# A two-layer decoder trunk on one core: boundary work reordered, level differences moved to VectorE

## The chip, the core and the metric

The kernel runs on one core of one Trainium2 chip. The metric is device time in microseconds (us), lower is better. The core has five engines that run side by side, each through its own list of instructions in order: TensorE (PE: matrix products into PSUM), VectorE (DVE), ScalarE (ACT), GpSimd (POOL) and SyncE (SP, which here only issues DMAs). They wait for each other by semaphores; `wait_ge(s, n)` holds an engine until `s` has reached `n`.

## The reference

Everything is float32. Batch 1, 512 tokens, width 1024, two layers. Cut to what matters:

```python
for l in range(2):
    mod = (silu(c) @ w_ada[l] + b_ada[l]).reshape(1, 3, 3, 1024)      # shift, scale, gate of 3 sub-layers
    x = modulated_sublayer(x, ffn1,         norm_g[l,0], norm_g[l,1], mod[:,0], 0.5)
    x = modulated_sublayer(x, token_mixing, norm_g[l,2], norm_g[l,3], mod[:,1], 1.0)
    x = modulated_sublayer(x, ffn2,         norm_g[l,4], norm_g[l,5], mod[:,2], 0.5)

def modulated_sublayer(x, fn, g_pre, g_post, m, res_w):
    h = rms_norm(x, g_pre) * (1 + scale) + shift
    return x + res_w * gate * rms_norm(fn(h), g_post)
def swiglu_ffn(h, w_in, w_out):                                        # hidden width 2816
    a, b = split(h @ w_in, 2);  return (silu(a) * b) @ w_out
# token_mixing: h @ w_in (8832 columns), then three mixers, gates, h @ w_out.
# Mixer A (6 heads): a gated linear recurrence with decays exp(b[t] - b[s]).
```

## The kernel before, in words

**Precision.** Each float32 factor is split into a high part (rounded) and a low part (the rest), and one product becomes three on PE: high by high, low by high, high by low (`three`, lines L769 to L771). So each group of weights (2048 columns on 128 partitions, 1 MB) is loaded into `RAW[g % 2]`, rounded by ACT into `WH[g % 2]` (`high`, L1164; in quarters L1173) and subtracted by DVE into `WL[g % 2]` (`low`, L1562; in quarters L1573). SP loads group g when the low part of group g - 2 has been made. `used(g)` counts that PE has done with a group; `free(g)` says which `used` the rounding of group g waits for.

**FFN.** The first product has 22 groups (11 pairs i, with u = 0, 1) of 128 hidden columns each. Groups 0 and 1 are done together by `first_pair`, in two halves of 256 tokens; each later group is 48 products of 512 columns. When PE has done a group, ACT takes silu (L1272), DVE multiplies (L1597), makes the low part of the group two further on (L1562), and of the result (L1601); this is a *tile* (`ffn_tile`). PE's group n + 2 waits for the low part and for the gate made in tile n. The second product (`rows_product`) has 11 groups; it fills all eight PSUM banks, and its last two groups are done together, column by column, so that finished columns can go on.

**Modulation.** `mod` is a product with a single row, so it is done beside the FFNs: the 1024 rows of a 512-column chunk of `w_ada` come in eight transfers of 256 KB into four buffers `AW`, DVE sums them up into `AACC` (*pieces*: four instructions, L1610 and L1613, for each half chunk), PE adds up the partitions with four products by ones (`ada`, L832), DVE copies the result (L1620). FFN1 of a layer has 11 chunks, one for each pair of groups; FFN2 has 7 in layer 0 and 2 in layer 1. On SP the transfers of the pieces of tile n stand behind the loads of group n + 3, which wait for the low part that is made in tile n - 1.

**Boundary.** Between two sub-layers (five times, and a last one without a next input) the output is squared (ACT L1198, DVE adds pairs L1482), summed over partitions by PE with ones (L779), the root taken by ACT (`root`, L1179 and L1181), the residual added by DVE (L1494, L1498), the new x squared (ACT L1206) and summed (PE L786), its root taken, and the next input made (DVE `U` L1505, ACT `HH` L1211, DVE `HL` L1512), in two halves of the tokens, so that PE can begin with the first columns. So that the next weights can be rounded before PE is done with the last rows, the first two groups behind a boundary go into two extra pairs of buffers, `WXH` and `WXL` (`beside`, `halves_of`).

**Mixing.** After the pair of `first_pair` 35 more items of the input product, each in eight steps k = 0..7; each step has some products and beside them a step of a mixer. Head h of mixer A has its eight steps in the item of head h + 1: for each of seven levels POOL makes a difference (`AD`, L1968), ACT the exponentials (`AE`, L1325 and L1326), DVE the scaled factors (`KL` L1737, `QL` L1739), PE a product (L973), and DVE takes it up (`AS`, L1721). Then `merge` (4 groups) and the 4 groups of `w_out` by `rows_product`.

The order is written out by hand in each engine's program; nothing is scheduled by a planner.

## Time and profile before

| | |
|---|---|
| Time, median of 3 runs | 3120.86 us (3119.76 to 3122.25) |
| Profiled execution: its own time | 3121.1 us |
| Profiled execution: span of the instructions | 3119.3 us |
| PE busy | 2929.9 us, 94% of the span |
| DVE busy | 1541.3 us, 49% |
| ACT busy | 1005.0 us, 32% |
| POOL busy | 193.1 us, 6% |
| mean granted clock of TensorE | 0.975 of full |

PE is busy nearly all the time, so the time is what PE has to do plus the stretches in which it waits. The clock is granted at one of two levels, full (2.4 GHz) and half (1.2 GHz); "0.975" is a mean over the span. A group of the profile's rows names the line, the engine, the operation and output <- inputs, with busy time and mean duration; idle time of an engine is put down to what ended it.

### The profile page before, as it was taken

The page shows a single profiled execution, that of the slowest core. Times are in us where ns is not written, and L with a number is a line of the kernel's source. Part 1 is how long each engine was busy: PE and PEld are TensorE (multiplying, and loading weights), DVE is VectorE, ACT ScalarE, POOL GpSimd, SP SyncE. Part 2 cuts the span into 40 slices and gives each one's busy share as a digit, 9 for nine tenths or more (in the row PEclk, how much of TensorE's full clock was granted, in tenths as well). Part 3 has the DMA queues.
Part 4 walks back from the last instruction along what each step waited for, and adds up shares of the span by engine and source line. Part 5 has one row for each costly group of instructions (what it writes and reads, how often), then busy time and mean ns, then how long its engine had stood idle before and what let it go on. Part 6 is the DMA issues. An engine that isn't in the chain of part 4 may idle for free.

```text
span 3119.3 us, 40607 instructions
## 1 busy us (share of the span) xinstructions
PE 2929.9 (94%) x16999; PEld 2558.1 (82%) x16999; DVE 1541.3 (49%) x2236; ACT 1005.0 (32%) x1455; POOL 193.1 (6%) x188
## 2 busy tenths in 40 slices
PE   6999898989999988999989989899899999899998
PEld 5888897777788788889988879877777887888897
DVE  5555236777344446542255552477753554453323
ACT  3322124444422323222242221354443232332212
POOL 1000001221100020000000000021211002000000
PEclk7999999999999999999999999999999999999999
DMA  6555331222112233542226542222111232343321
GB/s 238 176 189 189 109 96 61 61 62 68 41 55 82 81 127 104 189 135 95 97 88 195 186 167 89 88 62 75 51 52 41 68 95 81 109 122 95 102 89 55
DMA packets 358854, 324.53 MB, mean 104 GB/s; under 512 B 12300, under 2 KB 305552, under 8 KB 357776
## 3 DMA queue, kind: packets, MB, share of 16 engines
q1 hardware_dynamic: 357136, 319.77, 32.4%
q8 instruction: 135, 2.21, 0.3%
q10 hardware_dynamic: 1536, 2.16, 0.2%
q14 instruction: 47, 0.39, 0.0%
HBM read 313.43 MB, written 6.29 MB: 102 GB/s over the span
## 4 chain that ended last, share of the span: by engine, by line
PE 85%; DVE 7%; ACT 3%; issue 2%; POOL 0%; ACTq 0%; DVEq 0%; POOLq 0%
PE PS L769 25%; PE PS L771 24%; PE PS L770 24%; PE PS L973 2%; PE PS L786 2%; DVE WL L1573 1%; PE PS L1048 1%; PE PS L1010 1%; PE PS L1070 1%; PE PS L1034 1%; PE PS L1025 1%; PE PS L1022 1%; PE PS L832 1%; ACT WH L1164 1%; PE PS L779 1%
## 5 line engine op out<-in xcount | busy, mean ns | idle before, releaser
L769 PE MATMUL PS<-HH,WH 128*128 128x512 f32 (+1 forms) x2512 | 974.3, 388 | 27.3 <-DVE WL L1562 10.3
L771 PE MATMUL PS<-HH,WL 128*128 128x512 f32 (+1 forms) x2512 | 948.7, 378 | 0.0
L770 PE MATMUL PS<-HL,WH 128*128 128x512 f32 (+1 forms) x2512 | 946.9, 377 | 0.0
L1562 DVE TENSOR_TENSOR WL<-RAW,WH 128x2048 fp32r<-128x2048 f32 x142 | 325.5, 2292 | 515.5 <-ACT WH L1164 515.5
L769 PEld LDWEIGHTS PS<-HH,WH 128*128 128x128 f32 x2512 | 475.7, 189 | 116.7 <-DVE WL L1573 13.7
L771 PEld LDWEIGHTS PS<-HH,WL 128*128 128x128 f32 x2512 | 475.0, 189 | 88.7
L770 PEld LDWEIGHTS PS<-HL,WH 128*128 128x128 f32 x2512 | 476.1, 190 | 82.0 <-issue 2.9
L1164 ACT ACTIVATE WH<-RAW 128x2048 fp32r<-128x2048 f32 x142 | 271.8, 1914 | 792.6 <-PE PS L771 792.6
L769 PE MATMUL PS<-GH,WH 128*128 128x256 f32 x1408 | 405.0, 288 | 18.2 <-DVE WL L1562 17.5
L771 PE MATMUL PS<-GH,WL 128*128 128x256 f32 x1408 | 403.7, 287 | 0.0
L770 PE MATMUL PS<-GL,WH 128*128 128x256 f32 x1408 | 403.3, 286 | 0.0
L769 PEld LDWEIGHTS PS<-GH,WH 128*128 128x128 f32 x1408 | 272.1, 193 | 19.6 <-DVE WL L1562 18.4
L771 PEld LDWEIGHTS PS<-GH,WL 128*128 128x128 f32 x1408 | 271.3, 193 | 0.0
L770 PEld LDWEIGHTS PS<-GL,WH 128*128 128x128 f32 x1408 | 270.9, 192 | 0.4
L1573 DVE TENSOR_TENSOR WL<-RAW,WH 128x512 fp32r<-128x512 f32 (+1 forms) x264 | 173.4, 685 | 145.0 <-ACT WH L1173 144.5
L1597 DVE TENSOR_TENSOR SB<-SB,PS 128x512 f32<-128x512 f32 x88 | 60.5, 687 | 336.2 <-PE PS L771 336.2
L1613 DVE SCALAR_TENSOR_TENSOR AACC<-AW,CC,AACC 128x512 f32<-128x512 f32 x217 | 162.9, 751 | 20.8 <-DVE AACC L1613 0.9
L1173 ACT ACTIVATE WH<-RAW 128x512 fp32r<-128x512 f32 (+1 forms) x264 | 145.9, 601 | 82.9 <-PE PS L771 53.1
L1272 ACT ACTIVATE SB<-PS 128x512 f32<-128x512 f32 x88 | 52.7, 599 | 266.0 <-PE PS L771 261.0
L769 PE MATMUL PS<-HH,WXH 128*128 128x256 f32 x320 | 98.5, 308 | 23.4 <-DVE HL L1512 23.4
L1968 POOL TENSOR_TENSOR AD<-AB 128x512 f32<-128x512 f32 x84 | 97.1, 1173 | 184.0 <-ACT AE L1326 103.9
L973 PEld LDWEIGHTS PS<-QL,KL 128*64 128x64 f32 (+6 forms) x672 | 76.0, 177 | 38.2 <-DVE QL L1739 29.1
(225 smaller groups left out, 3470.3 us busy)
## 6 DMA issues: line engine op xcount, KB each, us to landing
RAW<-in_ffn_w_in SPq DMA_DIRECT2D x176, 512.0 KB, 5.2
RAW<-in_w_in SPq DMA_DIRECT2D x132, 512.0 KB, 4.7
AW<-in_w_ada SPq DMA_DIRECT2D x248, 256.0 KB, 4.8
RAW<-in_ffn_w_out SPq DMA_DIRECT2D x88, 512.0 KB, 4.2
AWB<-in_w_ada SPq DMA_DIRECT2D x5, 2048.0 KB, 16.0
RAW<-in_w_out SPq DMA_DIRECT2D x16, 512.0 KB, 4.0
x_kept<-X SPq DMA_DIRECT2D x2, 2048.0 KB, 7.4
X<-x_kept SPq DMA_DIRECT2D x2, 2048.0 KB, 10.1
```

The lines of the kernel that those rows point to most:

```text
L769: pe.matmul(o, ah, bh, start=start, stop=skip, skip_group_check=skip)
L770: pe.matmul(o, ah, bl, start=False, stop=skip, skip_group_check=skip)
L771: return pe.matmul(o, al, bh, start=False, stop=stop or skip, skip_group_check=skip)
L786: mm = pe.matmul(y_at(half, 0), ones, XSQ[q][:, e, :], start=(q == 0 and e == 0), stop=True, skip_group_check=True)
L973: mm = pe.matmul(PS[0:keys, 2 + n % 2, c * 64:(c + 1) * 64], KL[n % 2][:, c * P:c * P + keys], QL[n % 2][:, c, :], start=True, stop=True)
L1164: act.activation(halves_of(g)[0][:, 0:n], RAW[g % 2][:, 0:n], ACT.Copy).then_inc(w_high, 1)
L1173: act.activation(WH[slot][:, q * n:(q + 1) * n], RAW[slot][:, q * n:(q + 1) * n], ACT.Copy).then_inc(w_high if q == 3 else part_high, 1)
L1562: dve.tensor_tensor(wl[:, 0:n], RAW[g % 2][:, 0:n], wh[:, 0:n].bitcast(F32), ALU.subtract).then_inc(w_low, 1)
L1573: ins = dve.tensor_tensor(WL[slot][:, part], RAW[slot][:, part], WH[slot][:, part].bitcast(F32), ALU.subtract)
L1597: dve.tensor_tensor(SB[u][:, :], SB[u][:, :], PS[:, 2 * u + 1, :], ALU.mult).then_inc(gated, 1)
L1613: ins = dve.scalar_tensor_tensor(acc, w, CC[:, k:k + 1], acc, ALU.mult, ALU.add)
L1968: pool.tensor_tensor(level_view(AD[n % 2][:, :], k), b, b[:, :, w // 2 - 1:w // 2].broadcast_to([P, SEQ // w, w]), ALU.subtract).then_inc( ...
```

## The change

1. **The extra buffers** `WXH` and `WXL` now hold the last two groups of each `rows_product` (`beside`: `g % NG in HALVED`) and no longer the first two groups behind a boundary. Both last groups may be rounded from the use of the fourth last on. The third group behind a boundary (`g + 2`) now waits for the use of the first (in `first_pair`), where it waited for the end of the rows.
2. **Rows.** The first group of `rows_product` goes through the PSUM banks in another order, and each quarter waits only for its own banks. The columns of `ada` take banks 4 and 5 in turn.
3. **Modulation.** `ada(i)` stands behind group (i, 1) of its own pair i, where it stood one pair later (`ada(0)` behind group (1, 0)). On DVE the pieces of a tile stand in front of the tile, where they stood behind it.
4. **Boundary.** On ACT the squares of x come one step earlier among the squares of y; the second root of y is taken behind the first two columns of the next input. On PE the second sums of x come at steps 3, 4, 5, 5 of the first half, where they came at steps 4 to 7.
5. **Merging.** The low part of the first branch group is made in the last item, not behind it.
6. **Level differences.** The 84 differences `AD` are made by DVE and no longer by POOL; level k + 1 is made in step k.

SP's list of instructions is the same. PE has the same products, in another order.

```diff
@@ -439,12 +439,12 @@
     def beside(g):
-        return g % NG in (G_MIX, G_MIX + 1, G_FFN2, G_FFN2 + 1) or (g % NG < 2 and now[0] + g // NG > 0)
+        return g % NG in HALVED
     def free(g):
         if beside(g):
-            back = max((e for e in ROW_ENDS if e <= g), default=0) - 3
+            back = min(e for e in ROW_ENDS if e > g) - 4
         else:
@@ -809,8 +809,10 @@
                                 mm.then_inc(done(i), 1)
-                            if not half and p and (u, i) == (1, 1) and k >= KT // 2:
-                                x_sum(p, 1, k - KT // 2)
+                            if not half and p and (u, i) == (1, 1) and 3 <= k <= 5:
+                                x_sum(p, 1, k - 3)
+                                if k == 5:
+                                    x_sum(p, 1, 3)
                 def ffn_in(p, f, g0):
@@ -827,9 +829,9 @@
                         pe.wait_ge(ada_part, at(ada_part, i * KT + (ADA_BEFORE[f] + 2) * KT))
-                        pe.wait_ge(ada_out, at(ada_out, ADA_BEFORE[f] + i))
+                        pe.wait_ge(ada_out, at(ada_out, max(ADA_BEFORE[f] + i - 1, 0)))
                         for q in range(4):
-                            mm = pe.matmul(PS[:, 4, q:q + 1], AACC[i % 2][:, q * P:(q + 1) * P], ones[:, 0:1],
+                            mm = pe.matmul(PS[:, 4 + i % 2, q:q + 1], AACC[i % 2][:, q * P:(q + 1) * P], ones[:, 0:1],
                                            start=True, stop=True)
@@ -839,17 +841,16 @@
                             group(u)
-                            if u and i <= n:
-                                ada(i - 1)
-                    if n == FI // 2:
-                        ada(FI // 2 - 1)
-
-                def rows_product(g0, n, rh, rl, ready, b, bank_free=None):
+                            if (i, u) == (1, 0):
+                                ada(0)
+                            if u and i < n:
+                                ada(i)
+
+                def rows_product(g0, n, rh, rl, ready, b, bank_free):
                     def column(i, j, half):
-                        wh = WH[(g0 + i) % 2][:, :].rearrange("p (k c) -> p k c", k=2)
-                        wl = WL[(g0 + i) % 2][:, :].rearrange("p (k c) -> p k c", k=2)
+                        wh, wl = (w[:, :].rearrange("p (k c) -> p k c", k=2) for w in halves_of(g0 + i))
                         cols = HALVES[half]
@@ -859,9 +860,9 @@
                         ready(i)
-                        for half in (1, 0) if i == 0 else (0, 1):
-                            for j in range(KT):
-                                if i == 0 and bank_free:
+                        for half, j0 in ((1, 4), (0, 0), (0, 4), (1, 0)) if i == 0 else ((0, 0), (0, 4), (1, 0), (1, 4)):
+                            for j in range(j0, j0 + 4):
+                                if i == 0 and j == j0:
                                     bank_free(half, j)
@@ -899,6 +900,8 @@
                     def bank_free(half, j):
+                        if (half, j) == (1, 4):
+                            pe.wait_ge(x_done, at(x_done, 8 * b))
                         if half and j == 0:
@@ -1127,9 +1130,10 @@
                             mm.then_inc((br_done, w_used)[u], 1)
+                def merged_free(half, j):
+                    pe.wait_ge(br_mul, at(br_mul, {(1, 4): KT - 2, (0, 0): KT - 1}.get((half, j), KT)))
+
                 def merged(i):
-                    if i == 0:
-                        pe.wait_ge(br_mul, at(br_mul, KT))
                     pe.wait_ge(m_low, at(m_low, 2 * i + 2))
@@ -1146,7 +1150,7 @@
                     merge()
-                    rows_product(G_WO, 4, lambda k: HH[:, k, :], lambda k: HL[:, k, :], merged, 3 * l + 1)
+                    rows_product(G_WO, 4, lambda k: HH[:, k, :], lambda k: HL[:, k, :], merged, 3 * l + 1, merged_free)
                     ffn_in(3 * l + 2, 1, G_FFN2)
@@ -1239,14 +1243,16 @@
                         square_y(b, 1, q)
-                        if q in (1, 2) and not last:
-                            square_x(b + 1, 0, 2 * q - 2)
-                            square_x(b + 1, 0, 2 * q - 1)
-                    root_y(b, 1)
+                        if q < 2 and not last:
+                            square_x(b + 1, 0, 2 * q)
+                            square_x(b + 1, 0, 2 * q + 1)
                     if last:
+                        root_y(b, 1)
                         return
...
                         input_high(b + 1, 0, j)
+                        if j == 1:
+                            root_y(b, 1)
                         if j in (2, 4, 6, 7):
@@ -1582,13 +1588,13 @@
                         for u in range(2):
-                            ffn_tile(f, g0, i, u)
-                            if u == 0 and 1 < i <= n + 1:
-                                ada_columns(f, i - 2)
                             if i < n:
                                 ada_pieces(f, i, u)
-                    for i in range(min(n, FI // 2 - 2), n):
-                        ada_columns(f, i)
+                            ffn_tile(f, g0, i, u)
+                            if u == 0 and 1 <= i <= n:
+                                ada_columns(f, i - 1)
+                    if n == FI // 2:
+                        ada_columns(f, n - 1)
                 def ffn_tile(f, g0, i, u):
@@ -1617,7 +1623,7 @@
                     ch = i + ADA_FIRST if f == 0 else i + ADA_ALL - ADA_OWN if i < ADA_OWN else i - ADA_OWN
-                    dve.tensor_copy(MOD[:, 4 * ch:4 * ch + 4], PS[:, 4, 0:4]).then_inc(ada_out, 1)
+                    dve.tensor_copy(MOD[:, 4 * ch:4 * ch + 4], PS[:, 4 + i % 2, 0:4]).then_inc(ada_out, 1)
                 def take(m, i):
@@ -1713,6 +1719,16 @@
                         dve.tensor_tensor_scan(AB[h % 2][:, :], const("reset"), AB[h % 2][:, :], 0.0, ALU.mult, ALU.add).then_inc(p_log, 1)
+                def a_diff(h, k):
+
+                    n = A_LEVELS * h + k
+                    dve.wait_ge(p_log, at(p_log, 3 * h + 3))
+                    dve.wait_ge(v_decay, at(v_decay, max(n - 1, 0)))
+                    w = P >> k
+                    b = level_view(AB[h % 2][:, :], k)
+                    dve.tensor_tensor(level_view(AD[n % 2][:, :], k), b,
+                                       b[:, :, w // 2 - 1:w // 2].broadcast_to([P, SEQ // w, w]), ALU.subtract).then_inc(v_diff, 1)
+
                 def level_out(h, k):
@@ -1726,6 +1742,10 @@
                     aq, ab, ak, s = AQ[h % 2], AB[h % 2], AK[h % 2], AS[h % 2]
+                    if k == 0:
+                        a_diff(h, 0)
+                    if k + 1 < A_LEVELS:
+                        a_diff(h, k + 1)
                     if k < A_LEVELS:
@@ -1924,9 +1944,10 @@
                                 low_part(m + 1, k - 1)
+                            if (m, k) == (NM - 1, 3):
+                                low(G_BR)
                             mixers(m, k)
                     take(NM - 1, 1)
-                    low(G_BR)
                     low(G_BR + 1)
@@ -1958,25 +1979,12 @@
             def _(pool):
-                def a_diff(h, k):
...
                         pool.tensor_tensor(QB[h % 2][:, :], AQ[h % 2][:, :], AK[h % 2][:, :], ALU.mult).then_inc(i_qk, 1)
-                    if k < A_LEVELS:
-                        a_diff(h, k)
-
                 def mixers(m, k):
```

The next two pieces are DVE's rows in FFN1 of layer 0, pair i = 1: `SB` is the gated product of a tile, `WL` the weights' low part, `GL` the result's; `AACC<-AW` are the pieces of a chunk. Before:

```order
L1597 TENSOR_TENSOR SB_73<-SB_73,PS 128x512 [waits w_used,silu_done]
L1562 TENSOR_TENSOR WL_56<-RAW_52,WH_54 128x2048 [waits w_high]
L1601 TENSOR_TENSOR GL<-SB_73,GH 128x512 [waits g_high]
L1610 TENSOR_SCALAR AACC_80<-AW_75,CC 128x512 [waits ada_sum,ada_in0]
L1613 SCALAR_TENSOR_TENSOR AACC_80<-AW_76,CC,AACC_80 128x512 [waits ada_part,ada_in1]
L1613 SCALAR_TENSOR_TENSOR AACC_80<-AW_78,CC,AACC_80 128x512 [waits ada_part,ada_in2]
L1613 SCALAR_TENSOR_TENSOR AACC_80<-AW_79,CC,AACC_80 128x512 [waits ada_part,ada_in3]
L1597 TENSOR_TENSOR SB_74<-SB_74,PS 128x512 [waits w_used,silu_done]
L1562 TENSOR_TENSOR WL_57<-RAW_53,WH_55 128x2048 [waits w_high]
L1601 TENSOR_TENSOR GL<-SB_74,GH 128x512 [waits g_high]
L1613 SCALAR_TENSOR_TENSOR AACC_80<-AW_75,CC,AACC_80 128x512 [waits ada_part,ada_in0]
```

and now:

```order
L1616 TENSOR_SCALAR AACC_80<-AW_75,CC 128x512 [waits ada_sum,ada_in0]
L1619 SCALAR_TENSOR_TENSOR AACC_80<-AW_76,CC,AACC_80 128x512 [waits ada_part,ada_in1]
L1619 SCALAR_TENSOR_TENSOR AACC_80<-AW_78,CC,AACC_80 128x512 [waits ada_part,ada_in2]
L1619 SCALAR_TENSOR_TENSOR AACC_80<-AW_79,CC,AACC_80 128x512 [waits ada_part,ada_in3]
L1603 TENSOR_TENSOR SB_73<-SB_73,PS 128x512 [waits w_used,silu_done]
L1568 TENSOR_TENSOR WL_56<-RAW_52,WH_54 128x2048 [waits w_high]
L1607 TENSOR_TENSOR GL<-SB_73,GH 128x512 [waits g_high]
L1626 COPY MOD<-PS 128x4 [waits ada_sum]
L1619 SCALAR_TENSOR_TENSOR AACC_80<-AW_75,CC,AACC_80 128x512 [waits ada_part,ada_in0]
L1619 SCALAR_TENSOR_TENSOR AACC_80<-AW_76,CC,AACC_80 128x512 [waits ada_part,ada_in1]
L1619 SCALAR_TENSOR_TENSOR AACC_80<-AW_78,CC,AACC_80 128x512 [waits ada_part,ada_in2]
L1619 SCALAR_TENSOR_TENSOR AACC_80<-AW_79,CC,AACC_80 128x512 [waits ada_part,ada_in3]
```

The four pieces stood behind `SB`, `WL` and `GL` of their tile, and now stand in front of them; so `WL` for the group two further on stands behind waits for four transfers (`ada_in0` to `ada_in3`).

ACT at the boundary between FFN1 and mixing (`YSQ` and `XSQ` are the squares of y and x, `NLN` and `NR_103` the root for y, `NR_104` that for x, `HH` the next input, `WXH` the extra buffers). Before:

```order
L1198 ACTIVATE YSQ<-PS 128x2x256 [waits y_done] x2
L1206 ACTIVATE XSQ_93<-X 128x512 [waits n2_mm,x_done]
L1206 ACTIVATE XSQ_94<-X 128x512 [waits n2_mm,x_done]
L1198 ACTIVATE YSQ<-PS 128x2x256 [waits y_done]
L1206 ACTIVATE XSQ_95<-X 128x512 [waits n2_mm,x_done]
L1206 ACTIVATE XSQ_96<-X 128x512 [waits n2_mm,x_done]
L1179 ACTIVATE NLN<-PS,EPSC 128x256 [waits n2_mm]
L1181 ACTIVATE NR_104<-NLN 128x256 [waits n2_ln]
L1198 ACTIVATE YSQ<-PS 128x256 [waits y_done]
L1179 ACTIVATE NLN<-PS,EPSC 128x256 [waits n1_mm]
L1181 ACTIVATE NR_103<-NLN 128x256 [waits n1_ln]
L1211 ACTIVATE HH<-U,MOD 128x256 [waits u_done] x3
```

and now:

```order
L1202 ACTIVATE YSQ<-PS 128x2x256 [waits y_done]
L1210 ACTIVATE XSQ_93<-X 128x512 [waits n2_mm,x_done]
L1210 ACTIVATE XSQ_94<-X 128x512 [waits n2_mm,x_done]
L1202 ACTIVATE YSQ<-PS 128x2x256 [waits y_done]
L1210 ACTIVATE XSQ_95<-X 128x512 [waits n2_mm,x_done]
L1210 ACTIVATE XSQ_96<-X 128x512 [waits n2_mm,x_done]
L1202 ACTIVATE YSQ<-PS 128x2x256 [waits y_done]
L1183 ACTIVATE NLN<-PS,EPSC 128x256 [waits n2_mm]
L1185 ACTIVATE NR_104<-NLN 128x256 [waits n2_ln]
L1202 ACTIVATE YSQ<-PS 128x256 [waits y_done]
L1215 ACTIVATE HH<-U,MOD 128x256 [waits u_done] x2
L1183 ACTIVATE NLN<-PS,EPSC 128x256 [waits n1_mm]
```

Each two squares of x (`XSQ`) stand one square of y earlier, and the second root for y (`NLN` and then `NR_103`) stands behind the first two `HH`.

DVE in the first steps of head 0 of mixer A (`AD` the differences, `KL` and `QL` the scaled factors), now; before, no `AD` stood in DVE's rows:

```order
L1729 TENSOR_TENSOR AD_125<-AB_115 128x512 [waits v_decay,p_log]
L1729 TENSOR_TENSOR AD_126<-AB_115 128x512 [waits v_decay,p_log]
L1757 TENSOR_TENSOR KL_129<-AK_117,AE_127 128x4x64 [waits p_k,kl_set,p_q,v_mm,v_decay]
L1759 TENSOR_TENSOR QL_131<-AQ_113,AE_127 128x256
L1767 TENSOR_TENSOR KD<-AB_115 128x512 [waits i_turn,p_log]
L1771 TENSOR_TENSOR AS_133<-PS,CT 128x512 [waits i_o,i_diag]
L1579 TENSOR_TENSOR WL_57<-RAW_53,WH_55 128x256 [waits part_high,i_s0]
L1729 TENSOR_TENSOR AD_125<-AB_115 128x512 [waits v_decay,p_log]
L1757 TENSOR_TENSOR KL_130<-AK_117,AE_128 128x8x32 [waits p_k,p_q,v_mm,v_decay]
L1759 TENSOR_TENSOR QL_132<-AQ_113,AE_128 128x256
L1776 TENSOR_TENSOR QB_135<-AQ_113,EB 128x512 [waits i_eb]
```

Two differences stand ahead of the first factors, and then one ahead of each level's.

## Rows read from the trace of the kernel before

**Rows 1.** The page, busy time of each engine.

```profile
PE 2929.9 (94%) x16999; PEld 2558.1 (82%) x16999; DVE 1541.3 (49%) x2236; ACT 1005.0 (32%) x1455; POOL 193.1 (6%) x188
```

**Rows 2.** Who waited for whom, PE, 95 to 3119: total us, times, longest us.

```profile
PE PS L769 <- DVE WL L1562: 34.2, 9, 4.4
PE PS L769 <- DVE HL L1512: 23.4, 11, 2.6
PE PS L973 <- DVE AS L1721: 18.8, 12, 2.0
PE PS L832 <- DVE MOD L1620: 15.2, 2, 7.6
PE PS L786 <- ACT XSQ L1206: 12.1, 10, 1.2
...
PE PS L769 <- issue: 6.6, 2, 3.3
```

**Rows 3.** PE in order of time, four places.

```profile
330.49 1.84 PE L832 MATMUL PS<-CT,AACC 128*128 128x1 f32 x8 [7.60 <-DVE MOD L1620]
...
480.75 0.36 PE L769 MATMUL PS<-HH,WXH 128*128 128x256 f32 x1 [2.02 <-DVE HL L1512]
...
1072.97 0.77 PE L769 MATMUL PS<-YH,WH 128*128 128x512 f32 x1 [3.19 <-DVE WL L1562]
...
1380.69 0.47 PE L769 MATMUL PS<-HH,WH 128*128 128x512 f32 x1
```

**Rows 4.** Busy us by stretch; the column after POOL is granted clock.

```profile
442.30:450.30 8.00, 7.97 (x47) 7.98 (x48) 2.30 (x1) 3.39 (x4) 0.00 (x0) 0.67 0.90 260
...
3075.30:3083.30 8.00, 7.98 (x54) 7.98 (x55) 0.00 (x0) 1.56 (x3) 0.00 (x0) 0.79 0.00 0
330.50:340.50 10.00, 9.65 (x53) 9.60 (x54) 0.76 (x6) 0.00 (x0) 0.00 (x0) 0.61 0.33 120
1858.90:1868.90 10.00, 9.65 (x63) 9.60 (x64) 0.76 (x6) 0.00 (x0) 0.00 (x0) 0.74 0.32 119
1073.00:1081.00 8.00, 8.00 (x23) 6.35 (x24) 2.29 (x1) 0.00 (x0) 0.00 (x0) 0.63 0.79 262
480.80:488.80 8.00, 7.97 (x53) 7.68 (x54) 7.89 (x19) 2.92 (x7) 0.00 (x0) 0.79 0.00 1
500.20:508.20 8.00, 8.00 (x67) 8.00 (x68) 6.50 (x14) 5.47 (x8) 0.00 (x0) 1.00 0.00 0
```

**Rows 5.** SP in order of time, FFN1 of layer 0: issues of transfers.

```profile
95.64 1.00 SPq L688 DMA_DIRECT2D RAW<-in_ffn_w_in  x2
...
134.98 2.90 SPq L680 DMA_DIRECT2D AW<-in_w_ada  x4
```

**Rows 6.** DVE in order of time, FFN1 of layer 0: start us, us [idle before].

```profile
99.10 0.68 DVE L1597 TENSOR_TENSOR SB<-SB,PS 128x512 f32<-128x512 f32 x1
99.69 2.28 DVE L1562 TENSOR_TENSOR WL<-RAW,WH 128x2048 fp32r<-128x2048 f32 x1
...
131.60 2.29 DVE L1562 TENSOR_TENSOR WL<-RAW,WH 128x2048 fp32r<-128x2048 f32 x1 [1.25 <-ACT WH L1164]
...
135.06 1.61 DVE L1613 SCALAR_TENSOR_TENSOR AACC<-AW,CC,AACC 128x512 f32<-128x512 f32 x2
```

**Rows 7.** Tile AW, the four transfers issued from 134.98 on.

```profile
DMA to landing us min/median/max: 4.6/4.8/5.2
```

**Rows 8.** Line L832 on PE (ada), FFN2 of layer 0, seven chunks.

```profile
L832 PE MATMUL PS<-CT,AACC x56: 164/250/250, 1243.6 to 1380.6; 128*128 128x1 f32 x56
```

**Rows 9.** DVE in order of time, start of FFN1 of layer 1.

```profile
1624.56 0.49 DVE L1610 TENSOR_SCALAR AACC<-AW,CC 128x512 f32<-128x512 f32 x1 [0.76 <-DMA AW<-in_w_ada]
```

**Rows 10.** The page: rounding on ACT.

```profile
L1164 ACT ACTIVATE WH<-RAW 128x2048 fp32r<-128x2048 f32 x142 | 271.8, 1914 | 792.6 <-PE PS L771 792.6
```

**Rows 11.** The page, level differences on POOL.

```profile
L1968 POOL TENSOR_TENSOR AD<-AB 128x512 f32<-128x512 f32 x84 | 97.1, 1173 | 184.0 <-ACT AE L1326 103.9
```

**Rows 12.** Line L1739, whole run: duration ns min/median/max.

```profile
L1739 DVE TENSOR_TENSOR QL<-AQ,AE x84: 407/417/1326, 529.4 to 2281.3; 128x256 f32<-128x256 f32 x84
```

More of the change, by code:

```diff
@@ L1960, in _ @@
             def _(pool):
-                def a_diff(h, k):
-                    n = A_LEVELS * h + k
-                    pool.wait_ge(p_log, at(p_log, 3 * h + 3))
-                    pool.wait_ge(v_decay, at(v_decay, max(n - 1, 0)))
-                    w = P >> k
-                    b = level_view(AB[h % 2][:, :], k)
-                    pool.tensor_tensor(level_view(AD[n % 2][:, :], k), b,
-                                       b[:, :, w // 2 - 1:w // 2].broadcast_to([P, SEQ // w, w]), ALU.subtract).then_inc(v_diff, 1)
                 def a_head(h, k):
```

## The prediction

> **What bounds the kernel now.** I read the table of busy times first: PE works 94% of the span [rows 1]. So a change pays by what it takes out of PE's waits and costs what it adds there. Next, PE's waits [rows 2]: low parts `WL` end 34.2 us of them in nine waits, `HL` behind the boundaries 23.4 us, `AS` in mixing 18.8 us, `MOD` 15.2 us in two waits of up to 7.6 us, `XSQ` 12.1 us, and 6.6 us in two waits are "issue" (in front of `w_out`). PE in order of time places some: 7.60 us at the end of FFN1's first product, 2.02 us in front of the first half of the next input, 3.19 us in front of merging [rows 3]. Two of the nine waits for `WL` are this last kind; six of 4.4 us stand at the second last group of each `rows_product`. Last, the granted clock behind such waits [rows 4]: over 8 us it is 0.67 behind the first row end and 0.79 behind the sixth (mean of six: 0.71), over 10 us 0.61 and 0.74 behind the two waits of 7.6 us, 0.63 behind the merge wait, 0.79 behind the boundary wait of 2.02 us, and 1.00 behind the next half's. The granted clock is a mean between full and half level, so a stretch T at clock c has lost (1 - c) x T.
>
> **Extra buffers at the row ends: minus 40.1.** The second last group of `rows_product` may now be rounded from the use of the fourth last on, and its rounding and low part lie beside a whole group of products. Six times 4.39 = 26.3 us goes, and the clock's loss behind, 6 x 0.29 x 8 = 13.8. The last group's parts have the same cover, so nothing is late next.
>
> **Other boundary edits: minus 47.0.** With the squares a step earlier and the sums at steps 3 to 5, the `XSQ` waits go, 12.1. With the second root behind two columns of `HH`, the halves of the next input start earlier: of the 2.02 and 2.60 us (five boundaries; they make nearly all of the 23.4 us of `HL`) I take 3.4 off each boundary, 17.0, and leave 1.2 for the chain root, `U`, `HH`, `HL` of a first column. The dips behind the 2.02 us waits, 0.21 x 8 = 1.7 each, mostly go: 6.0. In front of merging `low(G_BR)` is already made: 2 x 2.3 of 2 x 3.19 goes (4.5) and the clock behind, 2 x 0.37 x 8 = 5.8. At `w_out` PE waits for its banks by quarters: 6.6. Sum 52.0. Against it, the third group behind a boundary has no cover by the rows any more: in the mixing its rounding and low part wait for the use of the first and queue behind other work of items 0 and 1 (ACT's copies of `QF` among it). The nearest row is the row-end wait, 4.39: I put 2.5 on each layer, bounds 0 and 4.4. 52.0 - 5.0 = 47.0.
>
> **Modulation pieces in front of the tiles: plus 105.3.** On this term the forecast rests. Four `AACC` now stand in front of `SB`, `WL`, `GL` of tile n. SP's order is the same: their transfers stand behind the load of group n + 3, which goes out when the low part of tile n - 1 is made (in tile 0 that is at 95.6; the load's issue is at 95.64 [rows 5]). So far `WL` stood in front of the sums and the transfers could land beside PE's products. Now `WL` of tile n stands behind them, and a loop closes: low part, transfers, sums, low part. Its length: a low part ends at 131.60 + 2.29 = 133.89 [rows 6]; the four issues go out from 134.98 to 137.6 (four in 2.90 us [rows 5]), and each lands 4.6 to 5.2 later [rows 7]: 6.3 behind the low part the first, 8.3 the last. The last sum takes 0.8 (two take 1.61 [rows 6]), so 9.1; `SB` holds DVE for 0.6 (99.10 to 99.69 [rows 6]), `WL` 2.29: with the gaps between them 12.4 to 12.6 for a tile, and I take 25.0 for a pair. PE's own pair is 22.7: seven chunks of `ada` begin at 1243.6 and end at 1380.69, the last eight products taking 0.8 [rows 3, 8], (1380.69 - 0.8 - 1243.6) / 6. So DVE's loop is the bound wherever pieces are made, by 2.3 a pair. In addition PE itself now stands at `ada(i)` behind group (i, 1) until the sums of tile 2i + 1 are there: group 2i + 2 starts 10.7 behind the low part of tile 2i (9.1, then the last sum's gap and 0.8 for `ada`).
> FFN1, layer 0: low part of tile 18 at 95.6 + 9 x 25.0 = 320.6, group 20 from 331.3, two more groups 22.7 (the last transfers wait for no load), rows from 354.0. They began at 330.49 + 1.84 + 0.35 = 332.7 [rows 3], a wait of 7.60 included, which this takes in. Plus 21.3. FFN1, layer 1: the same, and its first transfers go out late: even before they held the first sum for 0.76 us at 1624.56 [rows 9], and now they go out behind the third group's low part: 3.6 for that and 1.8 for the later low part, plus 26.7. FFN2, layer 0: six pairs at 2.3 = 13.8, and 11.5 for start and end: the third group's low part waits for the use of the first (a quarter group, 2.8, before the pair's end; rounding 1.91 [rows 10], low part 2.29, then sums and `SB` of tile 0: 5.1 us of wait), and the last `ada` is waited for. Plus 25.3. FFN2, layer 1, with two chunks: 2.3 + 11.5 = 13.8. Sum 87.1.
> The clock: the dips behind the two waits of 7.6 go, 10 x (0.39 + 0.26) = 6.5. Four new waits of 7 to 11 us at starts and ends cost 3.2 each by the same rows, 12.7. And each pair has a wait near 2.1 us, a length behind which the clock fell in one case and stayed in another [rows 4]. Over 27 pairs that is 0 to 27 x 1.7 = 46; near the lower end, since part of such a loss hides in the loop's slack, I take 12. 87.1 - 6.5 + 12.7 + 12 = 105.3.
> The page "DMA: Bandwidth & Descriptors" of the Trainium skill, section "Anatomy of one DMA — SWDGE (gpsimd) path", gives a transfer, issued by GpSimd, a fixed part of about 2 us besides bytes over a rate; were SP's like it, an estimate from it is 2.6 us for 256 KB, and the loop would fit into PE's time. The trace disagrees for SP's: 4.6 to 5.2 us [rows 7].
>
> **Level differences on DVE: minus 12.** POOL's 84 take 1173 ns each [rows 11]. As DVE instructions they should take what its other 512-column products take, 0.6: 50 us of DVE, which is 49% busy [rows 1], beside PE. What goes is POOL's step at the head of each level and what it does to its neighbours: `QL` takes 417 ns, and up to 1326 in some cases [rows 12]. The waits for `AS`, 18.8 us, stand in these heads. I take 12 of them off; bounds 0 (the chain is as long as before, now on DVE) and 20.
>
> **Sum.** 105.3 - 40.1 - 47.0 - 12.0 = +6.2. The profiled execution's own time is 3121.1 us, 0.2 over the median of 3120.86: 3127.3, so 3127. The bounds (loop 0.3 a pair, that is 8; dips up to 34 more; differences 10; boundaries 8) make 3114 to 3141 for this case.
>
> **Rivals.**
> A. The loop is as long, but neither its waits of two microseconds nor those at the starts lower the clock. For: 1.00 behind a wait of 2.60 [rows 4]. Against: every longer wait in rows 4 has a low clock behind it. 3127 - 12 - 12.7 = 3102. Chance 0.24.
> B. The transfers land in time, since with free buffers SP issues them one after the other and not over 2.9 us; the loop then fits into 22.7. The FFN term falls to four starts of 5.1 + 1.7, the waits of 7.6 go as well: 3121.1 - 40.1 - 47.0 - 12 - 13.2 - 6.5 + 27 = 3029, say 3030. Against: landings are some 0.65 apart while issues are 0.85 apart [rows 5, 7], so it is the amount in the queue that holds them. Chance 0.08. The rule of the Trainium skill named above would come out here.
> C. The clock falls in nearly every pair: 27 x 1.7 = 46 where I take 12, of which the loop's slack hides some 14: 3127 + 20 = 3147. It decides from the point at which a wait of 2.1 us always costs what it did behind the boundary (0.79 [rows 4]). Slower. Chance 0.13.
> D. DVE becomes the path in mixing: each level starts behind one more instruction, 84 x 0.6 = 50, of which 38 show, with no gain of 12: 3127 + 12 + 26 = 3165. For: 12 waits end on `AS` already. Against: POOL's step was twice as long. Chance 0.04.
> E. As forecast, 3127. Chance 0.51.
> Faster and slower mean by more than 0.2%, 6.2 us, about what a measurement of this kernel can tell from no change: below 3114.7 or above 3127.1. A, B and 0.03 of E are faster, 0.35; C, D and 0.28 of E slower, 0.45; the rest of E is the same, 0.20. The range, 3096 to 3150, leaves out B, D and the outer parts of A and C.
>
> **What the changed profile would show.** In the FFNs `AACC` with idle time ended by DMA `AW`; low parts 12.5 apart; PE's pairs 25.0 apart where pieces are made, with waits at `ada`; rows of FFN1 in layer 0 from about 354. No waits for `WL` at the row ends and none for `XSQ`; about 1.2 us in front of the first pair; the maximum of `QL` near 0.42 us. The forecast is wrong if those pairs are still 22.7 apart (B), if every one has a low clock (C), or if the `AS` waits have grown (D).

## The result, and the profile after

The changed kernel takes 3202.39 us (median of 4 runs, 3198.43 to 3208.80), the kernel before 3120.31 beside it: a ratio of 1.0264, 95% interval 1.0245 to 1.0284. That is 82 us slower. The forecast was 3127, with a range from 3096 to 3150.

The page of the changed kernel, busy times; the row of before is [rows 1]:

```profile
span 3196.6 us, 40607 instructions
PE 2966.0 (93%) x16999; PEld 2576.7 (81%) x16999; DVE 1542.2 (48%) x2320; ACT 1009.7 (32%) x1455; POOL 96.0 (3%) x104
```

PE has the same 16999 instructions and is busy 36 us longer: part of the loss is a lower clock, not waiting. PE's waits after (total us, times, longest), which answer to [rows 2]:

```profile
PE PS L834 <- DVE AACC L1619: 102.0, 25, 11.8
PE PS L769 <- DVE SB L1603: 19.3, 3, 9.0
PE PS L976 <- DVE AS L1737: 12.5, 12, 1.2
PE PS L769 <- DVE HL L1518: 10.1, 5, 2.0
...
PE PS L769 <- DVE WL L1568: 2.2, 2, 1.5
...
PE PS L769 <- issue: 1.7, 2, 0.8
```

What was to go is gone: the waits for `WL` (34.2 to 2.2), all those for `XSQ` (12.1), most "issue", more than half of `HL`. In their place stands one line: 25 waits of `ada` (L834) for `AACC`, 102.0 us, and 19.3 us in three waits for `SB` at the starts of FFNs.

I cut both spans at PE's first product of each stage. Lengths in us:

| Stage | before | after | difference |
|---|---|---|---|
| first products of the four FFNs | 261.9, 255.1, 268.0, 250.3 | 315.0, 300.6, 321.0, 267.0 | +168.3 |
| rows and boundaries behind them | 148.1, 147.0, 146.3, 148.0 | 133.5, 134.6, 133.5, 142.0 | -45.8 |
| merging, twice | 51.8, 51.7 | 45.6, 45.6 | -12.3 |
| `w_out` and its boundary, twice | 66.2, 66.1 | 53.8, 53.8 | -24.7 |
| mixing, twice | 592.2, 591.6 | 591.6, 584.5 | -7.7 |

The granted clock of these first products (busy us of each engine in a stretch; the number behind POOL is the clock). Before, FFN1 of layer 0 and 1:

```profile
70.80:332.70 261.90, 252.44 (x1243) 214.17 (x1241) 151.92 (x195) 75.34 (x82) 0.00 (x0) 0.98 0.55 177
...
1593.10:1861.10 268.00, 257.12 (x1257) 218.03 (x1257) 158.80 (x209) 77.82 (x87) 0.00 (x0) 0.98 0.54 173
```

and after:

```profile
70.30:385.30 315.00, 273.57 (x1242) 227.69 (x1241) 148.64 (x191) 74.20 (x82) 0.00 (x0) 0.92 0.45 144
...
1645.00:1966.00 321.00, 278.56 (x1259) 231.76 (x1257) 155.57 (x205) 78.02 (x88) 0.00 (x0) 0.92 0.44 141
```

The same products took 252.4 us of PE before and 273.6 now, at 0.98 and 0.92. Over the four stages PE's busy time rose from 1009.7 to 1074.0 us, 64.3 more for the same products, and the rest of 168.3, 104.0, is more waiting. The half level (1.2 GHz) stood for 25.6 us before and 160.4 us after. PE was busy in 13.6 and in 134.7 us of that; half of the difference, 60.6, is work that was not done in them, nearly the 64.3. Half-level time in which PE waits costs nothing.

Now one pair of tiles. DVE in order of time after, FFN1 of layer 0 (start, us; in brackets the idle time before it and what ended it):

```profile
226.36 0.49 DVE L1616 TENSOR_SCALAR AACC<-AW,CC 128x512 f32<-128x512 f32 x1 [6.00 <-DMA AW<-in_w_ada]
227.00 2.46 DVE L1619 SCALAR_TENSOR_TENSOR AACC<-AW,CC,AACC 128x512 f32<-128x512 f32 x3 [0.15 <-DMA AW<-in_w_ada]
230.80 0.69 DVE L1603 TENSOR_TENSOR SB<-SB,PS 128x512 f32<-128x512 f32 x1 [1.34 <-PE PS L771]
232.74 2.29 DVE L1568 TENSOR_TENSOR WL<-RAW,WH 128x2048 fp32r<-128x2048 f32 x1 [1.25 <-ACT WH L1168]
...
241.48 3.32 DVE L1619 SCALAR_TENSOR_TENSOR AACC<-AW,CC,AACC 128x512 f32<-128x512 f32 x4 [5.78 <-DMA AW<-in_w_ada]
244.71 0.68 DVE L1603 TENSOR_TENSOR SB<-SB,PS 128x512 f32<-128x512 f32 x1
...
260.27 0.69 DVE L1603 TENSOR_TENSOR SB<-SB,PS 128x512 f32<-128x512 f32 x1 [3.23 <-PE PS L771]
262.21 2.29 DVE L1568 TENSOR_TENSOR WL<-RAW,WH 128x2048 fp32r<-128x2048 f32 x1 [1.25 <-ACT WH L1168]
```

SP's issues, and PE's product by ones, in the same pair:

```profile
235.06 1.00 SPq L688 DMA_DIRECT2D RAW<-in_ffn_w_in  x2
```

```profile
244.85 1.58 PE L834 MATMUL PS<-CT,AACC 128*128 128x1 f32 x8 [3.28 <-DVE AACC L1619]
```

The even low part ends at 232.74 + 2.29 = 235.03, at 235.06 SP issues the next load, and the transfers behind it land for the first sum at 241.48 (6.45 later; I had 6.3). The sums end at 244.80, `ada` follows at 244.85. So far it is as forecast (+9.8 where I had 9.1). But then the even tile does not wait for DMA: its `SB` waits 3.23 us for PE (260.27). PE had begun group 2i + 2 only behind `ada`, and the clock fell:

```profile
235.00:245.00 10.00, 6.72 (x31) 5.25 (x30) 3.91 (x8) 2.51 (x2) 0.00 (x0) 1.00 0.67 210
245.00:260.00 15.00, 15.00 (x56) 12.32 (x57) 5.93 (x7) 1.23 (x2) 0.00 (x0) 0.77 0.44 140
260.00:275.00 15.00, 11.67 (x55) 9.45 (x53) 7.34 (x10) 4.99 (x5) 0.00 (x0) 1.00 0.44 141
```

It was 0.77 over the 15 us behind a wait of 3.28. The next low part ends at 264.50: 29.5 us for this pair, where I had 25.0. Added up along PE it is 11.4 from the low part to the end of `ada` (246.43), 13.8 for the group behind it (to about 260.2, where 10.9 is a group at the full level) and 4.3 for `SB`, rounding and low part. That the loop runs through `ada` and PE is here a reading; the experiments test it.

### The profile page after: what moved, and what is told of

Read it like the earlier page. It is cut to its first block and busy times, and to the rows that moved or that the text cites. A ratio compares the mean times of both kernels' runs of the same rounds, so it can differ in the third digit from the quotient of the medians.

```text
span 3196.6 us, 40607 instructions
## 1 busy us (share of the span) xinstructions
PE 2966.0 (93%) x16999; PEld 2576.7 (81%) x16999; DVE 1542.2 (48%) x2320; ACT 1009.7 (32%) x1455; POOL 96.0 (3%) x104
## 5 line engine op out<-in xcount | busy, mean ns | idle before, releaser
L769 PE MATMUL PS<-HH,WH 128*128 128x512 f32 (+1 forms) x2704 | 1053.3, 390 | 42.0 <-DVE SB L1603 19.3
L770 PE MATMUL PS<-HL,WH 128*128 128x512 f32 (+1 forms) x2704 | 1019.9, 377 | 0.0
L771 PE MATMUL PS<-HH,WL 128*128 128x512 f32 (+1 forms) x2704 | 1019.7, 377 | 0.0
L769 PEld LDWEIGHTS PS<-HH,WH 128*128 128x128 f32 x2704 | 525.1, 194 | 137.1 <-issue 25.4
L1168 ACT ACTIVATE WH<-RAW 128x2048 fp32r<-128x2048 f32 x140 | 268.0, 1914 | 692.9 <-PE PS L771 662.6
L771 PE MATMUL PS<-GH,WL 128*128 128x256 f32 x1152 | 326.2, 283 | 0.0
L770 PE MATMUL PS<-GL,WH 128*128 128x256 f32 x1152 | 325.6, 283 | 0.0
L769 PE MATMUL PS<-GH,WH 128*128 128x256 f32 x1152 | 324.1, 281 | 0.0
L769 PEld LDWEIGHTS PS<-GH,WH 128*128 128x128 f32 x1152 | 217.9, 189 | 0.1
L771 PEld LDWEIGHTS PS<-GH,WL 128*128 128x128 f32 x1152 | 217.3, 189 | 0.0
L770 PEld LDWEIGHTS PS<-GL,WH 128*128 128x128 f32 x1152 | 216.7, 188 | 0.1
L834 PE MATMUL PS<-CT,AACC 128*128 128x1 f32 x248 | 40.8, 286 | 102.0 <-DVE AACC L1619 102.0
L834 PEld LDWEIGHTS PS<-CT,AACC 128*128 128x128 f32 x248 | 39.3, 238 | 113.0 <-DVE AACC L1619 112.5
## 6 DMA issues: line engine op xcount, KB each, us to landing
X<-x_kept SPq DMA_DIRECT2D x2, 2048.0 KB, 10.9
```

The source lines that it names most:

```text
L769: pe.matmul(o, ah, bh, start=start, stop=skip, skip_group_check=skip)
L770: pe.matmul(o, ah, bl, start=False, stop=skip, skip_group_check=skip)
L771: return pe.matmul(o, al, bh, start=False, stop=stop or skip, skip_group_check=skip)
L834: mm = pe.matmul(PS[:, 4 + i % 2, q:q + 1], AACC[i % 2][:, q * P:(q + 1) * P], ones[:, 0:1], start=True, stop=True)
L1168: act.activation(halves_of(g)[0][:, 0:n], RAW[g % 2][:, 0:n], ACT.Copy).then_inc(w_high, 1)
```

## Experiments

The diffs are shortened; `...` stands for lines left out.

**E1: modulation as before, all else changed** (pieces behind tiles on DVE, `ada` one pair later on PE):

```diff
-                            if i < n:
-                                ada_pieces(f, i, u)
                             ffn_tile(f, g0, i, u)
...
+                            if i < n:
+                                ada_pieces(f, i, u)
...
```

> The changed kernel with the pieces behind their tiles and `ada` one pair later again (DVE and PE as before the change in the FFNs); boundary, merging, level differences as changed. In the changed kernel the four first products of the FFNs take 168 us more than before (53.0 + 45.5 + 53.0 + 16.7). Theory 1 (all of it but the FFN starts comes from where pieces and `ada` stand): back to 3202 - 168 + 4 starts of some 5 to 7 = about 3058, pairs at 22.7, the 7.6 us waits back. Rival (the FFN loss comes from the extra buffers moved to the row ends or the new bank order): still above 3150.

3041.56 us, ratio 0.974 (0.9715 to 0.9765). The rival falls: the FFNs' loss belongs to this one part. It came out 16 lower than theory 1 said, since the starts wait only 2.3 us each (6.8 in three) without pieces in front of tile 0.

**E2: only `ada` later.**

```diff
-                            if (i, u) == (1, 0):
-                                ada(0)
-                            if u and i < n:
-                                ada(i)
+                            if u and i <= n:
+                                ada(i - 1)
+                    if n == FI // 2:
+                        ada(FI // 2 - 1)
...
```

> The changed kernel with `ada(i)` one pair later again on PE, the pieces still in front of their tiles. Theory 1 (the loop that sets the pair runs through PE: low part of tile 2i, transfers, sums of tile 2i + 1, `ada(i)`, group 2i + 2, silu, rounding, low part: 10.7 + 10.9 + 4.3 = 25.9 at full clock, about 28.3 measured with the clock's dips): with `ada` out of it the loop on DVE alone is left, 25.0 a pair, so 27 x 3.3 = 89 less, about 3113 (3095 to 3130). Rival 2 (the loop on DVE and the transfers alone makes the 28.3, `ada` only shows it): 3202, pairs at 28.

3114.52 us, ratio 0.9973 (0.9963 to 0.9984), where theory 1 said 3113. Its waits:

```profile
PE PS L769 <- DVE WL L1568: 46.1, 40, 2.6
PE PS L769 <- DVE SB L1603: 19.5, 3, 9.2
...
PE PS L834 <- DVE AACC L1619: 8.1, 2, 4.7
```

The 102 us at `ada` became 46.1 us in 40 waits for `WL`, mean 1.15 us. DVE in order of time there:

```profile
216.76 0.49 DVE L1616 TENSOR_SCALAR AACC<-AW,CC 128x512 f32<-128x512 f32 x1 [7.00 <-DMA AW<-in_w_ada]
...
228.98 3.32 DVE L1619 SCALAR_TENSOR_TENSOR AACC<-AW,CC,AACC 128x512 f32<-128x512 f32 x4 [5.66 <-DMA AW<-in_w_ada]
...
242.52 0.48 DVE L1616 TENSOR_SCALAR AACC<-AW,CC 128x512 f32<-128x512 f32 x1 [6.82 <-DMA AW<-in_w_ada]
```

A pair is 242.52 - 216.76 = 25.8 and each tile waits for its own transfers. This is the loop that I had forecast for the changed kernel (25.0); it sets the pair only once `ada` is out of the way.

**E3: the transfers of the pieces in front of the load on SP.**

```diff
-                            if 2 * i + u + 1 < FI:
-                                group_after(2 * i + u + 1)
                             if i < chunks(l, f):
                                 if f == 0:
                                     pieces(i, u, own, ADA_FIRST)
                                 elif i < ADA_OWN:
                                     pieces(i, u, own, ADA_ALL - ADA_OWN)
                                 else:
                                     pieces(i, u, other, -ADA_OWN)
+                            if 2 * i + u + 1 < FI:
+                                group_after(2 * i + u + 1)
```

> The changed kernel, but SP issues the transfers of a tile's pieces in front of the load of group n + 3 and not behind it, so that they wait only for their buffers. Theory 1 (what the new order lacks is the transfers' head start): they go out before the low part and land under it; no wait at `ada`, pairs at 22.7, the 7.6 us waits gone too: 3202 - 168 - 13 + 4 starts of 5 to 7 = about 3040 (3025 to 3060). Rival (4 MB a pair in bursts, the queue's rate holds the loop whatever the order): above 3150.

3034.42 us, ratio 0.9719 (0.9697 to 0.9741). DVE's and PE's programs are those of the changed kernel, and yet all waits at `ada` are gone. PE's waits in the whole first product of layer 0 (85 to 323 us):

```profile
PE PS L769 <- DVE WL L1568: 1.5, 1, 1.5
```

`ada` in two pairs that follow each other there, 22.7 us apart and with no wait:

```profile
186.18 0.95 PE L834 MATMUL PS<-CT,AACC 128*128 128x1 f32 x8
208.88 0.95 PE L834 MATMUL PS<-CT,AACC 128*128 128x1 f32 x8
```

A low part of 1 MB and four sums fit well into PE's time; what the changed kernel lacked was the head start of its transfers. The queue's rate was not the limit.

**E4: the modulation part alone on the kernel before.**

```diff
...
-                            ffn_tile(f, g0, i, u)
-                            if u == 0 and 1 < i <= n + 1:
-                                ada_columns(f, i - 2)
                             if i < n:
                                 ada_pieces(f, i, u)
+                            ffn_tile(f, g0, i, u)
+                            if u == 0 and 1 <= i <= n:
+                                ada_columns(f, i - 1)
...
```

> The kernel before with the modulation part of the change alone: pieces in front of tiles, `ada` in its own pair with banks 4 and 5 in turn. Theory 1: the loop through `ada` costs as in the changed kernel, 168 less the starts that the moved extra buffers cost (about 20): 3121 + 148 = about 3269 (3250 to 3285). Rival (my forecast, loop of 25.0): about 3190.

3291.22 us, ratio 1.0541 (1.0524 to 1.0558), 169 slower; the same line stands on top:

```profile
PE PS L832 <- DVE AACC L1613: 103.6, 25, 11.9
```

It is 22 above theory 1: I had counted the FFN starts out, but FFN1 of both layers takes 318.6 and 325.3 us here, more than in the changed kernel.

**E12: more work on PE in front of `ada`**, to part the waits from the clock:

```diff
                             if u and i < n:
+                                for j in range(12):
+                                    pe.matmul(PS[:, 6, :], HH[:, 0, 0:P], HH[:, 1, :], start=True, stop=True)
                                 ada(i)
```

> The changed kernel with 12 products more on PE in front of each `ada(i)`, i from 1 on (512 columns each, some 2.7 us at the full level, into an unused bank, not read by anything). They fill the wait at `ada` and lengthen nothing, if the loop of 25.9 us a pair leaves 3.2 us to wait. In the changed kernel 160 us of the FFNs' first products stand at the half level, before 25; a half-level microsecond gives half the work, so this is 67 us of the 168. Theory (the low level follows the waits): with the waits filled the level stays up and the kernel with MORE work on PE is faster, about 3202 - 55 = 3147 (3135 to 3165). Rival (the low level follows the load, not the waits, or the clock isn't the price): 3202 or more; if the filler lies on the path, 3202 + 26 x 2.7 = 3272.

3168.25 us, ratio 1.0155 (1.0139 to 1.0170): 34 us faster than the changed kernel, with 324 products more. Its waits at `ada`, and FFN1 of layer 0:

```profile
PE PS L834 <- DVE AACC L1621: 34.3, 25, 8.9
```

```profile
70.30:371.30 301.00, 283.78 (x1360) 237.32 (x1359) 149.56 (x194) 76.83 (x83) 0.00 (x0) 0.98 0.47 151
```

The clock is back at 0.98 in this stage, and over the four first products the half-level time in which PE was busy fell from 134.7 to 48.6 us, which is worth 43. Both rivals fall. These stages became 35 us shorter: besides the 43 from the clock, PE's waiting fell by 68 us and the added products took 77.8 us of it, more than the waits that they filled. Two pairs there, without half-level time in them:

```profile
161.02 1.05 PE L834 MATMUL PS<-CT,AACC 128*128 128x1 f32 x8 [1.57 <-DVE AACC L1621]
187.52 1.05 PE L834 MATMUL PS<-CT,AACC 128*128 128x1 f32 x8 [0.80 <-DVE AACC L1621]
...
213.79 1.05 PE L834 MATMUL PS<-CT,AACC 128*128 128x1 f32 x8 [0.60 <-DVE AACC L1621]
239.98 1.05 PE L834 MATMUL PS<-CT,AACC 128*128 128x1 f32 x8 [0.51 <-DVE AACC L1621]
```

PE still waits at each, so the filler is not what sets the pair; at the full level the loop is 187.52 - 161.02 = 26.5 and then 239.98 - 213.79 = 26.2 us, where theory 1 had 25.9.

**The other parts, each alone on the kernel before.** E7 (extra buffers at the row ends):

```diff
-        return g % NG in (G_MIX, G_MIX + 1, G_FFN2, G_FFN2 + 1) or (g % NG < 2 and now[0] + g // NG > 0)
+        return g % NG in HALVED
...
```

> The kernel before with the extra buffers moved to the row ends and nothing else. By the prediction's terms: minus 40.1 at the row ends, plus 5.0 at the starts of mixing and about 8 at three FFN starts (2.3 each and clock): 3121 - 27 = 3094 (3086 to 3100). Rival (what the row ends give comes back whole at the next start): 3121.

3100.83 us, ratio 0.9936 (0.9921 to 0.9951), 18 less. By stages the rows and boundaries give 37 back, close to the 40 forecast; the starts behind them take 10.5 in the three FFNs and some 10 in mixing, where I had 13 in all. Of the 10 in mixing 5.4 is waiting, which is the term of 5.0; most of the rest is half-level time (13.7 and 21.7 us in the two mixings, 14.5 and 14.7 before).

E8 (boundary order):

```diff
-                        if q in (1, 2) and not last:
-                            square_x(b + 1, 0, 2 * q - 2)
-                            square_x(b + 1, 0, 2 * q - 1)
+                        if q < 2 and not last:
+                            square_x(b + 1, 0, 2 * q)
+                            square_x(b + 1, 0, 2 * q + 1)
...
+                        if j == 1:
+                            root_y(b, 1)
...
```

> The kernel before with the boundary order alone: squares of x one step earlier, their sums at steps 3 to 5, the second root of y behind two columns of the next input. By the prediction's terms: 12.1 + 17.0 + 6.0 = 35 less, 3086 (3080 to 3095). Rival (the other waits of the boundary take the place; only `XSQ` goes): 3109.

3087.89 us, ratio 0.9896 (0.9881 to 0.9911), 31 less. `XSQ` is gone and `HL` keeps 10.1 us in 5 waits of 2.0, where I had left 1.2 each:

```profile
PE PS L769 <- DVE HL L1516: 10.1, 5, 2.0
```

E9 (banks by quarters, low part in the last item):

```diff
...
+                            if (m, k) == (NM - 1, 3):
+                                low(G_BR)
                             mixers(m, k)
...
```

> The kernel before with the order of banks in the rows' first group, the waits by quarters, and the low part of the first branch group made in the last item. By the prediction's terms 4.5 + 5.8 + 6.6 = 17 less: 3103 (3098 to 3110). Rival (the next thing of the same place is as late): 3119.

3104.70 us, ratio 0.9946 (0.9932 to 0.9961), 16 less, as forecast.

E10 (level differences on DVE), alone, and E6, the changed kernel with E3's order but the differences on POOL:

```diff
+                    if k == 0:
+                        a_diff(h, 0)
+                    if k + 1 < A_LEVELS:
+                        a_diff(h, k + 1)
...
```

> The kernel before with the level differences on DVE and nothing else. My term was minus 12, and e3 against e6 measured minus 7: 3111 (3106 to 3116), waits for `AS` 12 instead of 19. Rival (DVE the longer path without the rest of the change): 3120 or more.

> As e3_sp_first, but the level differences made by POOL as before the change. My prediction's term: 12 slower than e3, 3046 (bounds 3034 to 3054), with the waits for `AS` back at 18.8 from 12.1. Rival (no effect): 3034.

E10: 3118.72 us, ratio 0.9993 (0.9983 to 1.0003), no difference that can be told. E6: 3041.64 against E3's 3034.42. That is 7 between the medians, but the four times of each overlap (3039.58 to 3047.01, 3029.15 to 3043.93), so what is shown is the wait and not the time. Waits for `AS`, first E6, then E3:

```profile
PE PS L976 <- DVE AS L1727: 19.2, 12, 2.0
```

```profile
PE PS L976 <- DVE AS L1737: 12.1, 12, 1.2
```

The wait is cut by 7, also in E10 (12.2 in 12). In E10 the half level in the two mixings stood for 42 us, before for 29: PE waited 6.9 us less in them and was busy 6.2 us longer, which covers the gain. How far this varies is told below.

**E5 and E11: what the changed kernel lacked, repaired.** E5 is E3 with the pieces of an FFN's first two tiles behind them:

```diff
-                            if i < n:
+                            if 0 < i < n:
                                 ada_pieces(f, i, u)
                             ffn_tile(f, g0, i, u)
+                            if i == 0:
+                                ada_pieces(f, i, u)
```

> As e3_sp_first, but the pieces of tiles 0 and 1 of each FFN stand behind their tiles. In e3 three FFN starts wait 5.2, 9.0 and 5.1 us for `SB` of tile 0. Theory (these waits are the sums in front of `SB`, 3.1 us each, and in FFN1 of layer 1 their late transfers, 6.7): they fall to 2.3 each, 12.4 us less and up to 4 of clock: about 3020 (3015 to 3026). Rival (the wait is the rounding and low part of the third group): no change, 3034.

3027.25 us, ratio 0.9698 (0.9680 to 0.9715): the lowest median here, 92 us under the kernel before and 175 under the changed one. Its waits for `SB`:

```profile
PE PS L769 <- DVE SB L1605: 6.8, 3, 2.3
```

They fell from 19.3 to 6.8 as expected; the median fell by 7 of the 12 to 16 us. In the profiled executions the first products of the FFNs became 10.8 us shorter, and the two mixings, which the edit does not touch, 5.9 us longer, with 27.3 us at the half level instead of 13.7.

E11 is E5 with the third group's low part behind the first `SB`:

```diff
                     inputs(b + 1, 1)
-                    low(g + 2)
+                    if b % 3 == 0:
+                        low(g + 2)
...
-                    if (i, u) != (0, 0) or (l, f) == (0, 0):
-                        low(g0 + 2 * i + u + 2)
+                    low(g0 + 2 * i + u + 2)
```

> As e5_first_behind, and at the three FFN starts behind a boundary the third group's low part stands behind the first `SB`, as in every other tile, and not in front of it. Three waits of 2.3 us for `SB` become 1.6 or less for the low part: 2 to 5 us less than 3027, 3024 (3018 to 3028). Rival: no difference that can be measured, 3027.

3029.49 us, ratio 0.9708 (0.9693 to 0.9723): no gain. The wait only changed its name and grew, to 4.0 us:

```profile
PE PS L769 <- DVE WL L1569: 13.6, 4, 4.0
```

ACT in order of time at such a start shows why:

```profile
1170.08 1.92 ACT L1168 ACTIVATE WH<-RAW 128x2048 fp32r<-128x2048 f32 x1 [4.17 <-PE PS L771]
1172.02 1.28 ACT L1272 ACT_TABLE_LOAD   x1
1173.31 0.60 ACT L1278 ACTIVATE SB<-PS 128x512 f32<-128x512 f32 x1
```

The silu stands behind the rounding and a table load of 1.28 us, so `SB` comes later than the rounded weights, and the low part had better go first.

## Why the prediction was wrong

**Modulation pieces: the step that failed.** I gave this term 105.3, it measured 168.3 in the changed kernel and 169 alone (E4). One part of its mechanism was right: the transfers wait for the low part of tile n - 1, the sums stand in front of the low part of tile n, and E3, which changes only the transfers' place on SP, takes all of it away. Two things in it were wrong: the path of the loop, and what the clock costs on that path.

The first is the path: "I take 25.0 for a pair", "DVE's loop is the bound wherever pieces are made". I worked out the loop on DVE and then hung `ada` on its end, as a delay for a group that has slack. But the group that waits for `ada` feeds the next even tile: low part, transfers, sums, `ada`, group, silu and rounding, low part. By my own rows this was 10.7 + 10.9 (a group) + 4.3 (`SB`, rounding, low part behind it), 25.9, longer than 25.0. E12 shows 26.2 to 26.5 for it at the full level, and E2 25.8 for the loop that I had. At the full level the way through PE is thus only some 0.5 us longer. Yet E2, which takes `ada` off it, brings 88 us: in the first products 39 of PE's busy time, which is the second point, and 50 of waiting, the first wait for `ada` of an FFN (11.8 us in FFN1 of layer 0) among it.

The second is the clock. I took 18.2 net (12 + 12.7 - 6.5), counting that "part of such a loss hides in the loop's slack". There is no slack: PE is on the loop, so half-level time in the group behind `ada` lengthens it, to 29.5 us in the pair shown. And the waits of pairs are not 2.1 us but over 3 (3.28 in the pair shown), a length behind which rows 4 show a low clock every time. Measured by PE's busy time the clock cost 64. E12 shows by adding work that the low clock follows the waits. So of the 63 us missed in this term, 46 are clock and 17 waits. This is rival C's mechanism. C had 46 us for 27 pairs, from 1.7 behind a wait of 2.02, and took 14 off for the slack. With the whole 46 the clock would have come to 46 + 12.7 - 6.5 = 52, near the 64.

**Extra buffers: nearly right.** All six waits went, and E7's rows and boundaries show 37 of 40.1. The price at the starts behind was mis-sized: 20 in E7 where I had 13 (5.0 in the prediction, 8 added before E7 ran). In the changed kernel three FFN starts waited 5.2, 9.0 and 5.1 us (19.3 in all); these I had: 5.1 inside the 11.5 for start and end, and 3.6 more in FFN1 of layer 1.

**Other boundary edits: right to a few us.** E8 gave 31 of 35.1, E9 16 of 16.9. The size that was off is the chain of a first column, 2.0 and not 1.2. Over all rows, boundaries, merging and `w_out` the stages gave 82.8 where the terms (without starts) said 92.1. The two mixings gave 7.7 where the terms come to 7 (12 less 5.0); that is partly luck, since the 12 was not reached (below).

**Level differences: half of it.** Minus 12 was forecast; 6 to 7 us of `AS` waits went (18.8 to 12.5, and 19.2 to 12.1 from E6 to E3), and no run shows more in the time. `QL` now takes 420 ns at the most, as forecast:

```profile
L1759 DVE TENSOR_TENSOR QL<-AQ,AE x84: 405/414/420, 568.6 to 2368.8; 128x256 f32<-128x256 f32 x84
```

The twelve waits did not vanish, they were shortened from up to 2.0 to 1.2. What they wait for is DVE's own list, before and after. DVE and POOL in front of such a wait (2.01 us) in the kernel before:

```profile
2102.70 2.76 POOL L1968 TENSOR_TENSOR AD<-AB 128x512 f32<-128x512 f32 x2 [0.21 <-issue]
2103.03 1.53 DVE L1756 TENSOR_TENSOR QB<-AQ,EB 128x512 f32<-128x512 f32 x1
2104.48 1.52 DVE L1758 TENSOR_TENSOR KD<-KD,AK 128x512 f32<-128x512 f32 x1
```

and DVE at the same place (a wait of 1.18 us) in the changed kernel:

```profile
2194.12 0.69 DVE L1776 TENSOR_TENSOR QB<-AQ,EB 128x512 f32<-128x512 f32 x1
2194.72 0.68 DVE L1778 TENSOR_TENSOR KD<-KD,AK 128x512 f32<-128x512 f32 x1
...
2195.92 0.68 DVE L1729 TENSOR_TENSOR AD<-AB 128x512 f32<-128x512 f32 x1
```

In front of all twelve waits, before and after, DVE works without a gap up to the `AS` that ends the wait, so its own instructions set it. Before, at six of them `QB` and `KD` ahead of that `AS` took 1.5 us each beside POOL's differences, and at the other six one `WL` took 1.3 to 1.5; after, each takes 0.7 or less. Against what this saves (1.7 us in the place shown) stands one `AD` of 0.68. So the gain came not from POOL's step at the head of the level but, as the prediction also said, from what it did to its neighbours.

**Rivals.** A and B fell: the clock fell in nearly every pair, and the transfers landed as before or later (median 5.2 us after, 4.9 before, in the same stage). D fell: the waits for `AS` became shorter, and E6 is not faster than E3.

## What to carry to other kernels

When an instruction that waits for a transfer is moved in front of one that feeds the critical engine, find out what lets the transfer go out; if that is the instruction now standing behind it, one iteration earlier, a loop has closed, and the order on the queue that issues it must move too. Follow such a loop through every engine, the busiest included, and take the longest way round. On that way a stall costs twice, once as a wait and once as the clock behind it (here 104 and 64 us).

## What the runs showed of the hardware

- Work added to an engine made the kernel faster: 12 products in front of each `ada`, where PE had mostly waited 3 to 4 us, held the granted clock at 0.98 instead of 0.92 in FFN1 of layer 0 and brought 34 us in all (E12).
- The half level is not bound to one place. In the changed kernel it stood for 20.5 us in the mixing of layer 0 and 3.4 us in that of layer 1, with stage times of 591.6 and 584.5 us; in E1, with the same mixing program, it was the other way round (3.4 and 20.5 us; 584.5 and 591.5). A difference of 7 us between two such kernels is thus within what one stage can do by itself, which is why the term of the level differences can't be read from the medians of E10 or of E6 and E3. The four executions of E3 alone took 3029.15 to 3043.93 us, at mean clocks of 0.987 to 0.981.
- With POOL at work on the level differences, DVE instructions of the same form took up to 1.53 us instead of 0.68. In the kernel before, `QB` on DVE takes 678/1101/1526 ns (shortest, median, longest of twelve); in E10, which only moves the differences to DVE, 681/683/685.
- The table load of 1.28 us on ACT at an FFN's start lies on the chain of the first tile (E11).
